# Weaving the small matmuls of two tiles together in a chunked delta-rule inverse, with one tile's chunks exchanged between partition halves

## The reference, cut to what matters

```python
def step(S, inp):
    r_t, w_t, k_t, v_t, kk_t, a_t = inp
    sa = -jnp.einsum('bhvk,bhk->bhv', S, kk_t)
    S = (S * w_t[:, :, None, :] + sa[..., None] * (kk_t * a_t)[:, :, None, :]
         + v_t[..., None] * k_t[:, :, None, :])
    return S, jnp.einsum('bhvk,bhk->bhv', S, r_t)
...
y = y + jnp.sum(r_h * k_h * f32(r_k), axis=-1, keepdims=True) * v_h     # the bonus term
```

## Time and profile before

| what | value |
|---|---|
| runs | 1195.26, 1196.15, 1196.45 us, median 1196.15 |
| profiled execution | 1195.98 us, span of the core 1194.3 us |
| PE busy over the span | 93% |
| rounds 0 to 7 | from 358.87 to 588.40 us after the span's start |
| DVE, ACT busy over the span | 35%, 29% |

### The profile page before, as it was taken

One profiled execution on the slowest core, in us unless ns is written; L12 is line 12 of the kernel. 1 busy time (PEld: TensorE's weight loads), 2 busy tenths in 40 slices (PEclk: granted clock), 3 DMA queues, 4 the chain that ended last, 5 costly groups with the idle time before them and its releaser, 6 DMA issues.

```text
span 1194.3 us, 25488 instructions
## 1 busy us (share of the span) xinstructions
PE 1109.1 (93%) x11088; PEld 1009.5 (85%) x11088; DVE 419.7 (35%) x914; ACT 349.4 (29%) x631; POOL 318.4 (27%) x200
## 2 busy tenths in 40 slices
PE   6799999999978888888799889999999999899995
PEld 5698889999866666666687679999999999899995
DVE  2400000291134757575634656532222222200003
ACT  4522222333323444444311223332232323111112
POOL 0554333343300000000111133334343343334340
PEclk9899999999978999999989689999999999999998
DMA  9865555234210000011123132222323323232311
GB/s 370 300 224 176 173 204 178 93 109 135 93 60 2 20 3 20 3 61 56 40 87 113 54 110 78 71 71 70 105 70 95 81 74 90 59 87 73 97 48 75
DMA packets 115884, 117.33 MB, mean 98 GB/s; under 512 B 5284, under 2 KB 102736, under 8 KB 112472
## 3 DMA queue, kind: packets, MB, share of 16 engines
q1 hardware_dynamic: 111296, 110.74, 29.0%
q10 hardware_dynamic: 4504, 5.36, 1.4%
HBM read 104.59 MB, written 11.49 MB: 97 GB/s over the span
## 4 chain that ended last, share of the span: by engine, by line
PE 82%; DVE 10%; DMA 2%; ACT 2%; issue 2%; SPq 1%; POOL 1%; DVEq 0%; ACTq 0%; POOLq 0%
PE ps L1408 78%; DMA ada_w<-in_w_ada 2%; PE ps L1728 1%; SPq L378 1%; DVE s_sb L1164 1%; DVE rsum L1165 1%; POOL w_lo L512 1%; PE ps L1621 1%; DMA gring<-g_d 0%; DVE XX L1124 0%; DVE Pb L1129 0%; DVE rsum L1172 0%; DMA kc_raw<-in_cache_attn_k 0%; PE ps L1960 0%; DVE y_sb L1401 0%
## 5 line engine op out<-in xcount | busy, mean ns | idle before, releaser
L512 POOL TENSOR_TENSOR w_lo<-w_raw,w_hi 128x2048 fp32r<-128x2048 f32 (+1 forms) x67 | 287.1, 4285 | 625.6 <-ACT w_hi L629 625.6
L1408 PE MATMUL ps<-hh,w_hi 128*128 128x274 f32 x1376 | 291.4, 293 | 5.1 <-DVE hl L988 3.5
L1408 PE MATMUL ps<-hh,w_lo 128*128 128x274 f32 x1376 | 289.5, 292 | 0.0
L1408 PE MATMUL ps<-hl,w_hi 128*128 128x274 f32 x1376 | 287.9, 290 | 0.0
L1408 PEld LDWEIGHTS ps<-hh,w_hi 128*128 128x128 f32 x1376 | 219.5, 190 | 11.4 <-issue 9.2
L1408 PEld LDWEIGHTS ps<-hl,w_hi 128*128 128x128 f32 x1376 | 219.4, 190 | 0.0
L1408 PEld LDWEIGHTS ps<-hh,w_lo 128*128 128x128 f32 x1376 | 219.1, 190 | 0.0
L629 ACT ACTIVATE w_hi<-w_raw 128x2048 fp32r<-128x2048 f32 (+1 forms) x67 | 119.3, 1780 | 115.0 <-PE ps L1408 110.6
L1408 PE MATMUL ps<-ah,w_hi 128*128 128x274 f32 x352 | 74.1, 292 | 3.8 <-DVE al L1380 3.8
L1408 PE MATMUL ps<-ah,w_lo 128*128 128x274 f32 x352 | 74.2, 292 | 0.0
L1408 PE MATMUL ps<-al,w_hi 128*128 128x274 f32 x352 | 74.0, 292 | 0.0
(11 more groups left out here) (355 smaller groups left out, 1569.0 us busy)
## 6 DMA issues: line engine op xcount, KB each, us to landing
w_raw<-in_w_ffn_in SPq DMA_DIRECT2D x44, 512.0 KB, 4.7
w_raw<-in_w_in SPq DMA_DIRECT2D x42, 512.0 KB, 4.9
ada_l<-in_w_ada SPq DMA_DIRECT2D x16, 1024.0 KB, 5.8
ada_w<-in_w_ada SPq DMA_DIRECT2D x8, 1024.0 KB, 14.1
w_raw<-in_w_ffn_out SPq DMA_DIRECT2D x16, 384.0 KB, 4.0
w_raw<-in_w_ffn_out SPq DMA_DIRECT2D x16, 320.0 KB, 3.4
g_d<-gst SPq DMA_DIRECT2D x16, 274.0 KB, 2.6
gring<-g_d SPq DMA_DIRECT2D x16, 274.0 KB, 2.8
```

The source lines that it names most:

```text
L512: pool.tensor_tensor(w_lo[:, s, 0:cols], w_raw[:, s, 0:cols], w_hi[:, s, 0:cols].bitcast(F32), ALU.subtract).then_inc(lo_done, 1)
L1408: return pe.matmul(out, lhsT, rhs, start=start, stop=stop)
```

## The change

1. **Turned tile.** For b (q = 1) the inverse's transpose `XT`, and with it `Pb` and `KC`, are kept with chunk c in the other half: `turned(q, c)` is the half. `p_level_p` and `p_cv` of b then read half c and write the other one, `p_level_x` and `p_wu` read the other half and write half c. So b uses the two quarters of the array that a leaves. To make b's operands this way, `p_scores(b)` has one more product (the third, `(bh, kt)`, goes to the exchanged halves, and is made again straight for `ATs`), and its transpose of `kt` becomes two matmuls against `ident`. The second result of `p_level_x(b)` moves to bank 5 (`x_turned`).
2. **Woven order.** `p_cv`, `p_level_p`, `p_level_x` and `p_wu` take both tiles: they wait for both, and issue block by block a, b, a, b (`each_block`). `p_level_x` issues first all blocks of the `X` part, then those of the `XT` part.
3. **Bonus.** `bonus(hp)` is split by halves of the frames: they go to the same bank (1), at slots 7 and 10, and DVE multiplies them in pieces k = 7 and k = 9 in place of k = 8. For the first pair of heads both are still made together, in two banks.

```diff
+        def turned(q, c):
+            return part[1 - c] if q else part[c]
+        def bonus_bank(hp, h):
+            return 4 if h and hp == 0 else 1
+        def x_turned(q):
+            return ps[:, 5, 6 * L:8 * L] if q else ps[:, 0, 2 * L:4 * L]
...
-                if k == 8:
-                    dve.wait_ge(bon_mm, hp + 1)
-                    for h in range(2):
-                        tt(z(1)[:, h * H:(h + 1) * H], ps[:, 1 + 3 * h, 0:H], z(2)[:, h * H:(h + 1) * H], ALU.mult)
+                if k in (7, 9):
+                    h = k // 9
+                    dve.wait_ge(bon_mm, 2 * hp + h + 1)
+                    i = tt(z(1)[:, h * H:(h + 1) * H], ps[:, bonus_bank(hp, h), 0:H], z(2)[:, h * H:(h + 1) * H], ALU.mult)
+                    if h == 0:
+                        i.then_inc(rk_done, 1)
...
-                for i, (x, y) in enumerate(((kh_, kt_), (kt_, bh_), (bh_, kt_), (bh_, rt_), (kh_, rt_))):
+                pairs = [(kh_, kt_), (kt_, bh_), (bh_, kt_), (bh_, rt_), (kh_, rt_)] + q * [(bh_, kt_)]
+                for i, (x, y) in enumerate(pairs):
...
-                            mm(bank(q, e)[part[c], i * L:(i + 1) * L], x[part[e], cols], y[part[e], cols])
-                for i, x in enumerate((kt_, bl_, kl_, v_)):
-                    ins = pe.transpose(bank(q, 2)[:, i * P:(i + 1) * P], x, ident[:, :])
+                            mm(bank(q, e)[turned(q, c) if i == 2 else part[c], i * L:(i + 1) * L],
+                               x[part[e], cols], y[part[e], cols])
+                if q:
+                    for c in range(2):
+                        mm(bank(q, 2)[turned(q, c), 0:P], kt_[:, c * L:(c + 1) * L], ident[:, :])
+                else:
+                    pe.transpose(bank(q, 2)[:, 0:P], kt_, ident[:, :])
+                for i, x in enumerate((bl_, kl_, v_)):
+                    ins = pe.transpose(bank(q, 2)[:, (i + 1) * P:(i + 2) * P], x, ident[:, :])
...
+            def each_block(tiles):
+                return [(n, n % 2, e, c) for e in range(2) for c in range(2) for n in tiles]
...
+            def p_level_p(tiles, lev):
+                for n in tiles:
...
+                        pe.wait_ge(lev_x[n % 2], lev_at(n, lev))
+                for n, q, e, c in each_block(tiles):
+                    ins = mm(bank(q, 2)[turned(q, c), (4 + e) * L:(5 + e) * L], ATs[q][part[c], e, :], X[q][part[c], e, :])
...
+            def p_level_x(tiles, lev):
+                for n in tiles:
+                    pe.wait_ge(lev_p[n % 2], lev_at(n, lev) + 1)
+                for n, q, e, c in each_block(tiles):
                     if lev < n_levels(n) - 1:
+                        mm(bank(q, 0)[part[c], e * L:(e + 1) * L], XT[q][turned(q, c), e, :], Pb[q][turned(q, c), e, :])
+                for n, q, e, c in each_block(tiles):
+                    k = turned(q, c)
+                    ins = mm(x_turned(q)[k, e * L:(e + 1) * L], Pb[q][k, e, :], XT[q][k, e, :])
...
+            def p_wu(tiles):
...
+                    ins = mm(bank(q, 2)[part[c], e * P:(e + 1) * P], XT[q][k, e, :], KC[q][k, e, :])
```

More of the change, by code:

```diff
@@ L757, in a_at @@
                 act.wait_ge(masked, n + 1)
-                act.activation(ATs[q][:, :, :], both_heads(q, 2, 1), ACT.Copy).then_inc(at_ev, 1)
+                act.activation(ATs[q][:, :, :], both_heads(q, 5 if q else 2, 1), ACT.Copy).then_inc(at_ev, 1)
             def a_cv(n):
@@ L1597, in _, with bonus @@
             pe.wait_ge(mod_ready, 1)
[L1599 to L1603, removed]
+            def bonus(hp, h):
+                pe.wait_ge(rk_done, 2 * hp + 1 + (h if hp else 0))
+                mm(ps[:, bonus_bank(hp, h), 0:H], bones[:, :], kl[:, h * H:(h + 1) * H]).then_inc(bon_mm, 1)
             def p_scores(n):
@@ L1633, in p_level_p @@
[L1633 to L1644, removed]
@@ new lines, in p_cv @@
+            def p_cv(tiles):
+                for n in tiles:
+                    pe.wait_ge(masked, n + 1)
+                    pe.wait_ge(tk_ev, n + 1)
+                for n, q, e, c in each_block(tiles):
+                    ins = mm(bank(q, 2)[turned(q, c), e * DH:(e + 1) * DH], CTs[q][part[c], e, :], tk[q][part[c], 2, part[e]])
+                    if e == 1 and c == 1:
+                        ins.then_inc(cv_mm, 1)
+            def p_level_p(tiles, lev):
+                for n in tiles:
+                    if lev == 0:
+                        pe.wait_ge(x0_done, n + 1)
+                        pe.wait_ge(at_ev, n + 1)
+                        pe.wait_ge(cv_ev, n + 1)
+                    else:
+                        pe.wait_ge(lev_x[n % 2], lev_at(n, lev))
+                for n, q, e, c in each_block(tiles):
+                    ins = mm(bank(q, 2)[turned(q, c), (4 + e) * L:(5 + e) * L], ATs[q][part[c], e, :], X[q][part[c], e, :])
+                    if e == 1 and c == 1:
+                        ins.then_inc(lev_p_mm[q], 1)
@@ new lines, in p_level_x @@
+            def p_level_x(tiles, lev):
+                for n in tiles:
+                    pe.wait_ge(lev_p[n % 2], lev_at(n, lev) + 1)
+                for n, q, e, c in each_block(tiles):
+                    if lev < n_levels(n) - 1:
+                        mm(bank(q, 0)[part[c], e * L:(e + 1) * L], XT[q][turned(q, c), e, :], Pb[q][turned(q, c), e, :])
+                for n, q, e, c in each_block(tiles):
+                    k = turned(q, c)
+                    ins = mm(x_turned(q)[k, e * L:(e + 1) * L], Pb[q][k, e, :], XT[q][k, e, :])
+                    if e == 1 and c == 1:
+                        ins.then_inc(lev_x_mm[q], 1)
@@ L1666, in p_chunks @@
+            def p_wu(tiles):
+                for n in tiles:
+                    pe.wait_ge(lev_x[n % 2], lev_at(n, n_levels(n)))
+                for n, q, e, c in each_block(tiles):
+                    k = turned(q, c)
+                    ins = mm(bank(q, 2)[part[c], e * P:(e + 1) * P], XT[q][k, e, :], KC[q][k, e, :])
+                    if e == 1 and c == 1:
+                        ins.then_inc(wu_mm, 1)
             def p_chunks(q, rows_, om, on):
@@ L1780, in _ @@
                 if u == 3:
-                    bonus(0)
+                    bonus(0, 0)
+                    bonus(0, 1)
             for g in range(16 * NR_):
@@ L1787, in _ @@
                 if p == 2:
-                    p_cv(a)
-                    p_cv(b)
+                    p_cv((a, b))
                 if 3 <= p < 13:
[L1791 to L1794, removed]
+                    (p_level_p, p_level_x)[(p - 3) % 2]((a, b), (p - 3) // 2)
+                if p in (7, 10) and rnd % 2 and rnd < NR_ - 1:
+                    bonus(rnd // 2 + 1, p // 10)
                 if p == 13:
-                    p_wu(a)
-                    p_wu(b)
+                    p_wu((a, b))
                 if p >= 14:
@@ L1837, in _ @@
             chain(1)
-            p_cv(NT)
+            p_cv((NT,))
             chain(2)
             for lev in range(4):
-                p_level_p(NT, lev)
+                p_level_p((NT,), lev)
                 chain(3 + lev)
@@ L1844, in _ @@
                     attn_tile(0, 0, 2)
-                p_level_x(NT, lev)
+                p_level_x((NT,), lev)
                 if lev == 3:
@@ L1848, in _ @@
             chain(7)
-            p_wu(NT)
+            p_wu((NT,))
             attn_tile(1, 0, 2)
```

35 lines of the change are left out of this document (5 added, 30 removed).

## The result

The changed kernel takes **1265.78 us** (median of 4 runs, 1259.06 to 1271.81) against 1196.06 for the one before: a ratio of 1.058 (95% interval 1.052 to 1.064), 70 us slower. The forecast was 1190, its range 1185 to 1240.

A forecast was written before the change was run, and what follows sets the result against it. PE (93% busy) was taken as the bound, alternating in the changed stage with waits for DVE. Rounds 2, 4, 6 give 1.5 us, rounds 1, 3, 5 give 4.2, the rest 0.4: 6.1 us, to 1190, range 1185 to 1240.

The forecast's parts named there:

- rival B: Changed stage: overlapped matmuls may not hold TensorE's clock, so it falls to half in many places; 1210 to 1240, chance 0.36.
- A: Whole kernel: the main forecast, weaving makes the stage 6.1 us shorter, 1190 us, own range 1187 to 1193; chance 0.46.
- B's size: Changed stage: 75 to 130 us at half clock, priced at 0.43 us each, costing 20 to 50 us; middle 1230.
- What weaving saves: PE in the woven steps: 3.97 us a round, 31.8 us of PE in 8 rounds.
- What it adds: PE at `p_scores(b)`: an extra product, two `kt` matmuls and a shape change, 0.33 to 0.57 us, taken as 0.45.
- The common wait: PE at 25 steps that already waited for `Pb` or the last `XX`: some 0.2 us more each, for b's delay.
- the replay of one round: Even round 4, slot by slot with delays and savings: ends 0.5 us earlier, all that is left of 3.97 saved.
- The odd round's: Odd rounds: half of the bonus leaves PE early, DVE has one product less before the last `Pb`; 1.4 us earlier.
- C: Woven steps: quarters don't overlap in the new order, nothing is saved; about +6 us, 1202, chance 0.06.
- D: Whole kernel: no change, common waits cost 0.3 us and `p_scores(b)` 0.57; 1195.5, chance 0.06.
- E: Whole kernel: faster still, the next pair's work closes gaps and even rounds give 1.5 us; 1186, chance 0.06.

The follow-up runs named there:

- e3: The changed kernel with each step called tile by tile again, each tile with its own wait, turned layout and split bonus kept: 1217 us.
- e2: The changed kernel with each woven group of blocks issued twice in a row, in the same order: 1240.05 us.
- e4: The changed kernel, woven and with common waits, but with tile b's layout straight, on the same two quarters as a: 1235 us.
- e5: The kernel before with only the split bonus (product in two halves at steps 7 and 10, DVE's reading in two): median 1202.61 us.
- e1: The changed kernel plus one unused 128x128 matmul after each of steps 3 to 12, fewer in odd rounds: 1244 us.
- e6: The turned layout called tile by tile (as e3) plus one unused 128x128 matmul after each of ten steps: even round 27.61 us, profiled execution 1213.38 us.
- e8: The kernel before with only the common wait for both tiles added in each of the 12 steps: 1.7% more median time, profiled run 1212.59 us.
- e7: The kernel before plus one unused 128x128 matmul after each of steps 3 to 12 (3 to 6 in odd rounds): even round 29.04 us at full clock.
- e12: The changed kernel with its layout and common waits, but each step's matmuls issued tile by tile instead of alternating: 1258 us.

## Why the prediction was wrong

**The step that failed** is the weighing of rival B, and in it the sentence "Against: no matmul is left out, and rounds 4 and 5, which hold `p_scores` and `p_out` in all four quarters, had 1.00 throughout". It kept B at 0.36 behind A. Those rounds had a few such steps; the change overlaps eleven more in each, and the clock fell in all eight rounds: 224 us of the stage at half clock for 9. The condition that B named ("if overlapped matmuls keep the clock up only as one would") fits the runs that change the stream: a shorter stream of the same blocks lowers it (e3), the same stream twice restores it (e2). It doesn't explain e4 and e5, which have 58 and 23 us at half clock without overlap between tiles.

**B's size** was wrong mainly in the time at half clock: 75 to 130 us were taken, 224 came, and this alone puts the result outside B's 1210 to 1240. The price of 0.43 us was read from rounds 0 and 4, which differ in more than the clock; rounds of e1 give 0.31 to 0.41. The 20 to 50 us of B were already less than 75 to 130 at 0.43, which is 32 to 56; 215 at 0.31 to 0.41 are 67 to 88. The Trainium skill ("TensorE: Matmul & The Clock Gate", "HAM oscillation — how this bites in real kernels") explains falls inside a kernel by gaps in which PE stands idle. Here that isn't enough: no wait of PE in the changed kernel's stage is over 1.3 us, and e2 waits more than it does (16.5 for 14.1 us on `Pb`, 7.4 for 3.6 on `XX` of L1153) and keeps its clock.

**What weaving saves.** `p_level_p` 0.22 and `p_cv` 0.22 (0.23 predicted), `p_wu` 0.42 (0.47): right. `p_level_x` 0.23 where 0.47 stood, four times, and nothing for the last one, because I gave its second result four quarters where it has two. So 2.7 us in place of 3.97. And the saving comes from the layout alone: one order or the other, a round with one filler has PE busy 26.40 (e1) and 26.44 us (e6).

**What it adds.** `p_scores(b)` runs from 515.49 to 517.11, 1.62 us for 1.30 before: +0.32, the low end of 0.33 to 0.57, where I took 0.45. The half-wide pair takes 0.37 us to the next start (516.35 to 516.72), a change of shape included: both at once.

**The common wait** was, beside the halved saving of `p_level_x`, the mis-sized term of the sum: "a wait of some 0.2 us" at the 25 steps that already waited, some 0.6 us a round. e8 measures 1.8 us an even round and 1.0 an odd one. PE's waits for DVE grew by 11.2 us over the stage, of it 4.7 for `Pb`, 3.1 for `XX` at steps that had hardly waited (4 waits before, 8 now), 2.1 for `BDs` at `p_cv`, and 1.3 for the last `XX`. The rule's 21 waits of 0.2 us for `Pb` are 4.2, near the 4.7; `XX` at the other steps and `p_cv` stand outside its 25 steps, and only the replay of one round took them up. Why it adds up to so much no run of its own shows; my reading is that each step's wait for b starts DVE's work on a later as well, and that the replay gave a part of each back by a saving that was half as large. With ten fillers in both, e1's even round is 0.56 us longer than e7's, where the sum had 0.5 less: A failed apart from the clock too, as far as rounds with fillers show it.

**The odd round's** split bonus was right: 0.8 us (e5) at an even clock. **C** (no overlap) is out, as the rows of e3 and of the kernel after show; the rule of the skill that stood beside it too, for these shapes. **D** and **E** didn't happen.

What stays open: what exactly the chip counts, why the clock falls in e4, and what the changed kernel would take at full clock. Shown is that matmul work added without touching layout and order brings the clock back (e1, e2), that idle time added to a short stream takes more of it (e12), and that busy share doesn't decide.

## What to carry to other kernels

Read the granted clock by window before making a matmul phase shorter: where a stage with gaps between its matmuls had one fall already, a cut in PE's streaming time there by overlap can cost more than it saves. Whether it pays first to shorten what PE waits for was not tried. To let one engine wait for two producers at once makes each step start with the later one (1.8 us an even round in e8). Write down for each block which rows and columns of the array it uses; one output that has to stay in place can undo half of the packing.

## What was not expected of the hardware

- Matmuls in different quarters overlapped, and their starts alternated in the records, though the program issued one tile's eight blocks ahead of the other's (e3, 581.48 to 581.78). The Trainium skill ("TensorE: Matmul & The Clock Gate", "Step-by-step: what each phase is for") says that matmuls stay in program order and only weight loads are pulled ahead; the starts in this trace don't show such an order across quarters.
- Two neighbours with the same rows and other columns overlap as well as those with other rows: `p_level_p` takes 0.46 us for 8 blocks in the woven kernel, 0.68 before.
- Issuing every woven block twice made the kernel 26 us faster than issuing it once (1240.05 for 1265.78 us).
- Runs of one and the same kernel differ by 8 to 15 us with the mean clock (e5: 0.970 with 1191.94 us, 0.954 with 1206.45).
